# Attention values of one window group projected token-major for all heads at the start of a layer

## What is computed

```python
for l in range(DEPTH):                                  # DEPTH = 2
    h = rms_norm(x, g_mix[l])
    z = h @ w_in[l]
    qa, ka, va, ga, ub, vb, qc, kc, vc, gates = split_cols(z)
    # A: retention on qa, ka, va, ga (4 heads of 128)
    # B: causal spatial gating on ub, vb
    # C: 3 window groups x 4 heads x 128, with normed q and k
    for gi, (win, dil) in enumerate(((128, 1), (512, 4), (2048, 16))):
        o, lse = dilated_window_attention(qc[:, :, gi], kc[:, :, gi], vc[:, :, gi], win, dil)
        ...
    wts = softmax(stack(lses)); yc = sum(wts * outs)
    x = x + merged(gates, ya, yb, yc) @ w_o[l]
    x = x + SwiGLU(rms_norm(x, g_ffn[l]))
```

## Time and profile before

| | |
|---|---|
| time, median of 3 runs | 1905.05 us (1904.66 to 1905.68) |
| time of the profiled execution | 1904.88 us |
| its span in the profile | 1903.1 us |
| busy: PE, DVE, ACT, POOL | 1889.8, 1241.8, 850.4, 96.9 us |
| clock granted to TensorE, mean | 1.0 of full speed |
| read from and written to HBM | 291.79 and 77.66 MB |

### The profile page before, as it was taken

The page is one execution under the profiler, slowest core; times in us unless marked ns, Lnnn a source line. Parts: engine busy times, 40 slices in busy tenths (PEclk is TensorE's granted clock), DMA queues, the critical chain, the costliest instruction groups (busy, mean ns, idle before and its releaser), DMA issues. The chain is left out here.

```text
span 1903.1 us, 26512 instructions
## 1 busy us (share of the span) xinstructions
PE 1889.8 (99%) x10600; PEld 1696.9 (89%) x10600; DVE 1241.8 (65%) x1617; ACT 850.4 (45%) x1190; POOL 96.9 (5%) x148
## 2 busy tenths in 40 slices
PE   8999999999999999999999999999999999999999
PEld 7888888888888899899888888888888888998998
DVE  7767746666566786377577677566665667863775
ACT  5544444444334464155335444444443344642554
POOL 0000001111111000000000000011111110000000
PEclk9999999999999999999999999999999999999999
DMA  5322347777787455366333222577777774653663
GB/s 203 94 75 71 86 114 206 193 195 197 200 213 208 125 177 174 100 191 197 122 100 95 68 78 80 143 191 194 207 199 197 210 195 128 189 160 104 201 211 123
DMA packets 85897, 295.68 MB, mean 155 GB/s; under 512 B 20368, under 2 KB 20624, under 8 KB 84624
## 3 DMA queue, kind: packets, MB, share of 16 engines
q1 hardware_dynamic: 73104, 218.49, 37.0%
q0 software_dynamic: 12672, 75.51, 17.5%
HBM read 291.79 MB, written 77.66 MB: 194 GB/s over the span
## 5 line engine op out<-in xcount | busy, mean ns | idle before, releaser
L1076 ACT ACTIVATE w_high<-raw 128x1024 fp32r<-128x1024 f32 x396 | 418.3, 1057 | 780.1 <-PE bank L851 651.0
L1284 DVE TENSOR_TENSOR w_low<-raw,w_high 128x1024 fp32r<-128x1024 f32 x396 | 483.0, 1222 | 142.8 <-ACT w_high L1076 136.1
L851 PE MATMUL bank<-h_high,w_high 128*128 128x512 f32 x1344 | 518.7, 386 | 9.0 <-DVE h_low L1289 8.2
L851 PE MATMUL bank<-h_low,w_high 128*128 128x512 f32 x1344 | 510.1, 380 | 0.0
L851 PE MATMUL bank<-h_high,w_low 128*128 128x512 f32 x1344 | 510.1, 380 | 0.0
L851 PEld LDWEIGHTS bank<-h_high,w_high 128*128 128x128 f32 x1344 | 254.7, 190 | 45.3 <-issue 8.2
L851 PEld LDWEIGHTS bank<-h_high,w_low 128*128 128x128 f32 x1344 | 254.5, 189 | 36.2
L851 PEld LDWEIGHTS bank<-h_low,w_high 128*128 128x128 f32 x1344 | 254.7, 189 | 35.1
L851 PE MATMUL bank<-in_high,w_high 128*128 128x512 f32 x672 | 255.4, 380 | 0.0
L851 PE MATMUL bank<-in_low,w_high 128*128 128x512 f32 x672 | 254.7, 379 | 0.0
L851 PE MATMUL bank<-in_high,w_low 128*128 128x512 f32 x672 | 254.7, 379 | 0.0
(11 more groups left out here) (166 smaller groups left out, 2451.7 us busy)
## 6 DMA issues: line engine op xcount, KB each, us to landing
raw<-weights SPq DMA_DIRECT2D x325, 512.0 KB, 4.2
weight_sums<-weights POOLq DMA_DIRECT2D x108, 512.0 KB, 6.5
raw<-weight_sums SPq DMA_DIRECT2D x72, 512.0 KB, 4.1
weight_sums<-weight_sums POOLq DMA_DIRECT2D x36, 512.0 KB, 4.0
turned<-rows SPq DMA_DIRECT2D x3, 768.0 KB, 7.4
xT<-x_t SPq DMA_DIRECT2D x8, 256.0 KB, 5.7
decay_sb<-decay SPq DMA_DIRECT2D x8, 256.0 KB, 4.0
out_t<-xT SPq DMA_DIRECT2D x8, 256.0 KB, 4.5
```

The lines of the kernel that those rows point to most:

```text
L851: return pe.matmul(o, w, m, start=start, stop=stop)
L1076: act.activation(w_high[:, PART_SLOT[s], :, :], raw[:, s % RAW_SLOTS, :, :], ACT.Copy).then_inc(part_high_w.sem, 1)
L1284: dve.tensor_tensor(w_low[:, PART_SLOT[s], :, :], raw[:, s % RAW_SLOTS, :, :], w_high[:, PART_SLOT[s], :, :], ALU.subtract).then_inc(part_ ...
```

## The change

The value tiles of group 0 (v0 of each head) leave the heads. Four token-major tiles `vz` at the very start of the layer project the group-0 values of all four heads at once, into both score banks, the output bank and one of the turn banks. Once the norm is known, ACT evacuates them to `vz` in SBUF, and the `pv` of group 0 reads them there. A head has eight tiles. `pre[t+12..14]` becomes `pre[t+13..15]` for `ptrans` and `pv`; `weigh` stays at t+11, which with eight tiles to a head is the fourth tile (q0) of the following head. Keys k0 of the first head lose their exception. The norm of a layer's input is computed after the third tile, and spread after the fourth. `rq 0` and `rk 0` go ahead of the `rv` tiles, whose banks change. At the start, SP loads the second slab before the last two parts of x, and ACT and DVE split it there. POOL, which waits for the evacuation of `rq 0`, starts its sums of weights four tiles earlier. The number of tiles stays the same.

```diff
 def tiles_of_layer():
     t = []
+    t += [("vz", j) for j in range(HEADS)]
     for h in range(HEADS):
         t += [("k", h, g) for g in range(N_GROUP)] + [("q", h, g) for g in range(N_GROUP)]
-        t += [("v", h, g) for g in range(N_GROUP)]
-    t += [("rv", j) for j in range(HEADS)]
+        t += [("v", h, g) for g in range(1, N_GROUP)]
...
     for h in range(HEADS):
-        t += [("rq", h), ("rk", h), ("rg", h)] + gated(2, [h])
+        t += [("rq", h), ("rk", h)] + [("rv", j) for j in range(HEADS) if h == 0] + [("rg", h)] + gated(2, [h])
...
-            pre[t + ((2, 4, 4) if h > 0 else (3, 4, 4))[j]] += [("rowstat", "ck", h, j), ("rowstd", "ck", h, j)]
+            pre[t + (2, 4, 4)[j]] += [("rowstat", "ck", h, j), ("rowstd", "ck", h, j)]
...
-        pre[t + 7] += [("scores", h, 0), ("scores", h, 1), ("expo", h, 0), ("vtrans", "v", h, 0)]
+        pre[t + 7] += [("scores", h, 0), ("scores", h, 1), ("expo", h, 0)]
         pre[t + 8] += [("scores", h, 2), ("scores", h, 3), ("expo", h, 1)]
         post[t + 8] += [("gather", h), ("swap", h)]
         pre[t + 11] += [("weigh", h)]
-        pre[t + 12] += [("ptrans", h, 0), ("ptrans", h, 1)]
-        pre[t + 13] += [("ptrans", h, 2), ("pv", h, 0), ("ptrans", h, 3)]
-        pre[t + 14] += [("pv", h, 1), ("pv", h, 2), ("high", "yc", h), ("low", "yc", h)]
+        pre[t + 13] += [("ptrans", h, 0), ("ptrans", h, 1)]
+        pre[t + 14] += [("ptrans", h, 2), ("pv", h, 0), ("ptrans", h, 3)]
+        pre[t + 15] += [("pv", h, 1), ("pv", h, 2), ("high", "yc", h), ("low", "yc", h)]
...
-        if i < AHEAD_OF_NORM:
-            assert not pre[i] and len(BLOCKS[i]) == KT
+        if TILES[i][0] == "vz":
             steps.append(("main", i, 0, KT))
...
+            if i == AHEAD_OF_NORM:
+                steps += [("stat", "n", 0), ("rstd", "n", 0)]
+            steps += splits + later
+            if i == AHEAD_OF_NORM + 1:
+                steps += [("bcast", "n", 0), ("keep_rstd", 0), ("token_evac", "vz")]
             continue
...
+            if role == "vz":
+                return score_bank + [out_bank, turn_bank[1]]
...
-            return [stat_bank, out_bank, bank_of(base, AT["rv", 0]), score_bank[0]]
+            return [stat_bank] + score_bank + [out_bank]
...
             for n in range(KT):
                 sp.dma_start(xT[:, n, :], x_in[:, n, :]).then_inc(x_loaded[n], 16)
-            load(0, 1)
+                if n == SECOND_SLAB_AT:      # SECOND_SLAB_AT = 5
+                    load(0, 1)
...
                 if role == "rv" and j == 0:
+                    pe.wait_ge(std_ready.sem, std_ready.at(base, "cq", HEADS - 1))
+                    pe.wait_ge(score_taken.sem, score_taken.at(base, "scores", HEADS - 1, 3))
                     pe.wait_ge(low_ready.sem, low_ready.at(base, "yc", HEADS - 2))
...
+                same = [u for u in range(i) if TILES[u][0] not in TOKEN_ROLES and bank_of(base, u) is bank_of(base, i)]
+                if same and first == 0:
+                    wait_evacuated(pe, base, same[-1])
...
-                        pe.wait_ge(v_stored.sem, v_stored.at(base, "v", h, g))
+                        if g == 0:
+                            pe.wait_ge(values_ready.sem, values_ready.at(base, "vz", BLK - 1))
+                        else:
+                            pe.wait_ge(v_stored.sem, v_stored.at(base, "v", h, g))
...
+                                v = v_tok[g][:, kb, :] if g > 0 else vz[kb][:, h * P:(h + 1) * P]
-                                last = matmul(o, v_tok[g][:, kb, :], probsT[:, n, :],
+                                last = matmul(o, v, probsT[:, n, :],
```

More of the change, by code:

```diff
@@ L152 @@
     PROJECTION_EVENTS += [("slab", b[0]) for b in _bs[:-1] if LAST_BLOCK[b[0]] == (_i, b)] + [(_i,)]
-TOKEN_ROLES = ("rv", "sv")
+TOKEN_ROLES = ("vz", "rv", "sv")
 SCALED_ROLES = {"rq", "rk", "v", "rg", "su", "gate", "fgate"}
@@ L215, in schedule @@
         pre[t + 11] += [("weigh", h)]
-        pre[t + 12] += [("ptrans", h, 0), ("ptrans", h, 1)]
-        pre[t + 13] += [("ptrans", h, 2), ("pv", h, 0), ("ptrans", h, 3)]
-        pre[t + 14] += [("pv", h, 1), ("pv", h, 2), ("high", "yc", h), ("low", "yc", h)]
+        pre[t + 13] += [("ptrans", h, 0), ("ptrans", h, 1)]
+        pre[t + 14] += [("ptrans", h, 2), ("pv", h, 0), ("ptrans", h, 3)]
+        pre[t + 15] += [("pv", h, 1), ("pv", h, 2), ("high", "yc", h), ("low", "yc", h)]
     for h in range(HEADS):
-        t = AT["rq", h]
-        post[t] += [("rotate", "rq", h)]
-        post[t + 1] += [("rotate", "rk", h)]
+        post[AT["rq", h]] += [("rotate", "rq", h)]
+        post[AT["rk", h]] += [("rotate", "rk", h)]
+        t = AT["rg", h] - 2
         pre[t + 3] += [("rscore", h, m) for m in range(2)]
@@ L278, in schedule @@
         later = [("split_low", s) for s in todo if FIRST_USE[s] > i]
-        if i < AHEAD_OF_NORM:
-            assert not pre[i] and len(BLOCKS[i]) == KT
+        if TILES[i][0] == "vz":
+            assert not pre[i] and not post[i]
             steps.append(("main", i, 0, KT))
[L282 to L285, removed]
-            continue
[L287 to L293, removed]
+            if i == AHEAD_OF_NORM:
[3 more added lines that the diff above has]
+                steps += [("bcast", "n", 0), ("keep_rstd", 0), ("token_evac", "vz")]
+            continue
+        if i in AFTER_NORM:
+            w = 1 + AFTER_NORM.index(i)
             steps += [("main", i, 0, KT)] + splits + later
@@ L298, in schedule @@
                       ("main", i + 1, BCAST_AT, KT)]
-        elif i - 1 not in AFTER_NORM[1:]:
+        elif i - 1 not in AFTER_NORM:
             steps.append(("main", i, 0, len(BLOCKS[i])))
@@ L309 @@
 STAT_AT, BCAST_AT = 3, 6
-AFTER_NORM = (AT["k", 0, 0], AT["fgate", 0, 0])
+AFTER_NORM = (AT["fgate", 0, 0],)
 AHEAD_OF_NORM = 2
+SECOND_SLAB_AT = 5
 STEPS = schedule()
@@ L389, in build @@
                       over("values_low", in_low_at + 10 * row_bytes, [P, 2, SEQ], F32)]
+        vz_rows = [over("first_values_high", in_high_at + 4 * row_bytes, [P, 2, SEQ], F32),
+                   over("first_values_low", in_low_at + 4 * row_bytes, [P, 2, SEQ], F32)]
+        vz = [vz_rows[m // 2][:, m % 2, :] for m in range(BLK)]
         ret_v = [ret_v_rows[m // 2][:, m % 2, :] for m in range(BLK)]
@@ L601, in wait_turn_bank @@
         def wait_turn_bank(pe, base, n):
+            if n == 1:
+                pe.wait_ge(values_ready.sem, values_ready.at(base, "vz", BLK - 1))
             if n < 2:
@@ L886, in by_token @@
                     k = 2 * j + kk
+                    if role == "vz":
+                        pe.wait_ge(low_ready.sem, low_ready.at(base, "h", 0, k))
+                        seen_inputs.add(("h", 0, k))
                     wh, wl = (in_turn(w[:, PART_SLOT[slab], 4 * kk:4 * kk + 4, :].rearrange("p c n -> p (c n)"))
@@ L889, in by_token @@
                     for b in range(BLK):
-                        if role == "rv" and k == 0 and b == BLK - 1:
-                            pe.wait_ge(score_taken.sem, score_taken.at(base, "scores", HEADS - 1, 2))
                         if role == "sv" and k == 0 and b == BLK - 1:
@@ L957, in score_target @@
                 n = S_USERS.index(user)
+                if user[0] == "rscore" and user[1] == 0:
+                    pe.wait_ge(values_ready.sem, values_ready.at(base, "rv", 2))
                 if n >= 2:
@@ L1091, in _ @@
                 high_of_x(h_high[:, n, :], n, first_gain)
-            split(0, 1)
+                if n == SECOND_SLAB_AT:
+                    split(0, 1)
             for n in range(KT):
@@ L1160, in _ @@
                         for b in range(BLK):
-                            dst, func = (ret_v[b], ACT.Copy) if role == "rv" else (sg_v[:, b, :], ACT.Gelu_apprx_tanh)
+                            dst, func = {"vz": (vz[b], ACT.Copy), "rv": (ret_v[b], ACT.Copy),
+                                         "sv": (sg_v[:, b, :], ACT.Gelu_apprx_tanh)}[role]
                             act.activation(dst, token_bank(base, role)[b][:, :], func, scale=rs[:, b:b + 1]).then_inc(
@@ L1668, in _weights @@
                     k, at = 2 * t[1] + i // 4, i % 4 * P
-                    values = w_in[layer][k * P:(k + 1) * P, of((t[0], 0)):of((t[0], 0)) + HEADS * P]
+                    col = of(("v", 0, 0) if t[0] == "vz" else (t[0], 0))
+                    values = w_in[layer][k * P:(k + 1) * P, col:col + HEADS * P]
                     values = values.reshape(P, 2 * P, 2).transpose(0, 2, 1).reshape(P, HEADS * P)
```

8 lines of the change are left out of this document (2 added, 6 removed).

## The result

| | before | changed | ratio (95% interval) |
|---|---|---|---|
| time, median | 1905.37 us (4 runs) | 1932.12 us (4 runs) | 1.014 (1.0128 to 1.0152) |
| span of the profiled execution | 1903.1 us | 1929.4 us | |

The change costs 26.8 us. The forecast had the direction and the wait, and missed 17 us: the time lies outside its range.

A forecast was written before the change was run, and what follows sets the result against it. PE's own instruction stream plus the start was taken to bound the kernel: 1904.88 - 3.5 (turning of v0) + 13.6 (six waits at stat q0) = 1915.0 us, with a range of 1906.5 to 1921.

The forecast's parts named there:

- Turned values: PE no longer turns v0: eight groups of four transposes go, 0.44 us each, 3.5 us saved.
- The chain from the end of q0 to its square: ACT and DVE links delay q0's square to 7.45 us; PE waits 2.27 us at stat q0, six times, 13.6 us.
- Next in line: After the wait, q1's square is done at about 14 us, before PE's stat q1 at 15.2; holds by 1 us.
- A: The moment at which PE has issued the last matmul of q0, from which the chain is counted.
- Rival 3: A further deadline slips (stat q1, pair swap or a DVE evacuation): up to 1 us more at six heads, 1915 to 1921; chance 0.12.
- The table load: ACT's load between the slab's high part and shift_exp begins only after the operation ahead ends; 1.37 us in each chain.
- The clock: PE's clock expected full, also in the six waits of 2.27 us; no cost in the sum.
- rival 4: The clock falls in the six waits, costing at least 1.9 us each: 1926 us; chance 0.07.
- The start, zero: First matmul stays at 8.24 us and nine matmuls still run at half clock; the changed start is worth nothing.
- Nothing late by POOL: POOL's sums, begun four tiles sooner beside the last head's swap, end in no PE wait; no cost.

The follow-up runs named there:

- experiment 1: Changed kernel with weigh moved from pre t+11 to post t+10, behind the evacuation of the k2 tile: 1903.18 us, 0.9991 of before.
- the filled kernel: Changed kernel with eleven extra matmuls on PE, whose product nothing reads, ahead of stat q0 in heads 1 to 3: 1917.91 us, ratio 1.0066 to before.
- experiment 8: Changed kernel with weigh in post t+10 and POOL's sums of weights begun at the evacuation of rg 0 instead of rq 0: 1903.40 us, 0.9988 of before.
- FILL = 6, 4 and 2: Changed kernel with six, four or two extra matmuls on PE ahead of stat q0 in heads 1 to 3: 1918.2, 1923.6 and 1928.7 us.
- experiment 4: Changed kernel with rowstat and rowstd of k0 moved to pre t+3, behind weigh, for heads 1 to 3: 1923.91 us, ratio 1.0096 to before.

## Why the prediction was right or wrong

- **Turned values, -3.5 us: right.** The group of value transposes has 64 where it had 96. Take every place where other work stands between two 512- or 256-column matmuls, and of the distance between these two what is more than one matmul: in PE's timeline this adds up to 131.7 us in experiment 1 and to 135.4 before, 3.7 less.
- **The chain from the end of q0 to its square: right.** It took 7.14 us against 7.13, and the wait of 2.2 us is 2.37 between starts, against 2.27, at the six places named. The 0.1 more is the last handover: PE resumes 0.15 us after the square's end (109.97 to 110.12), where my estimate was 0.06. In the sum: 6 x 2.37 = 14.2 for 13.6.
- **Next in line: right.** q1's square ended 13.6 us after A, which the forecast had at about 14, and PE had no wait at stat q1. Rival 3 did not occur there.
- **The table load: the row was right.** 103.90 is where the split ends and the load begins, and the exponential begins 0.02 us after the load. The Trainium skill (ScalarE: Activation LUTs, What ACT_TABLE_LOAD costs) gives a drain of about 1380 ns more for a switch. This case's traces don't agree: these rows leave no gap for it.
- **The clock: the step that failed.** The forecast took the clock as full in the waits, so the term for it in the sum was nothing. It had no ground for that: the text itself said that waits of 0.5 us don't exclude a fall for 2.3 us, and still gave rival 4 a chance of 0.07 and left it out of the range. The clock fell behind five of six waits, which cost 13.4 us by the profile and 14.2 against the filled kernel; the range ended 11 us short. Rival 4 had the mechanism and the place right and the size too small, 11.4 us: it priced all six at 1.9 and called that the least. Two falls cost 1.7, three 3.4, and one place had none.
- **The start, zero: right as far as it can be told.** The first matmul came at 8.21 us. Six matmuls ran at half clock where there had been nine, but 9 to 13 in the other profiles of this start, so this is chance. (The view of windows gives 1.00 for this stretch in every profile; only the distance between the matmuls shows the half clock there.)
- **Nothing late by POOL: wrong.** "End in no PE wait that I can find": the swap of the last head came late. In the changed kernel's profile DVE waits 8.15 us for it and PE loses 0.5 us. PE needs the result two tiles later, which is why so little came of it.
- **The 26.3 us between the profiles:** -3.5 (values), +14.2 (six waits), +0.4 (the second one-column matmul behind each wait starts 0.075 us late), +13.4 (half clock), +0.5 (last head), -0.6 (the start), and +0.9 for the stretch from the last matmul's start to the end of the span (4.6 against 3.7). That makes 25.3; most of the 1.0 left lies in steps of 0.1 to 0.3 us at places outside the windowed attention. Another 0.3 us of the time lies outside the span: 2.1 us where it was 1.8.
- **Open:** experiments 1 and 8 should have come to 1901.4 to 1901.6 and came to 1903.2 and 1903.4. About 0.6 of it is the base, a profiled execution of 1904.9 where the medians beside them were 1905.3 to 1905.5. Another 0.3 is the time outside the span, 2.1 or 2.2 us in every run of both and 1.7 or 1.8 in every run of before beside them. In their profiles the stretch behind the last matmul's start is 0.7 and 1.1 us longer than in that of before. But it is 3.7 us, as before, in the kernels with FILL = 6, 4 and 2 and in that of experiment 4, so the change doesn't force it. The half-clock start of experiment 8 has thirteen matmuls for nine (0.8 us). What sets these was not settled.

## What to carry to other kernels

In a kernel that one engine bounds, follow what each moved step is put *in front of* on every in-order engine: here an exponential and its table load slid ahead of a square for which PE waits, a tile later than before. Price a new wait of TensorE twice, once as time and once as clock: for six waits of 2.2 us in this kernel the second price (13.4 to 14.2 us) was about as large as the first (14.2 us). Where no row shows what a wait of the forecast length does to the clock, the range has to hold both cases. Where a wait can't be removed, check whether a shorter one or independent matmuls in it keep the clock.

## What the runs showed of the hardware

- One wait of TensorE of 0.9 us left the granted clock at 2.4 GHz in 6 places of 6. Behind one of 1.3 us it fell to 1.2 GHz in 3 of 6, behind 1.5 us in 6 of 6, 1.8 us in 6 of 6, 2.2 us in 5 of 6; behind three waits of 0.8, 0.4 and 0.2 us within 3.4 us in 3 of 6. Each count is of one execution. Ahead of each, PE had run without a pause, and behind or between them came one-column matmuls. Whether the clock would fall without these was not tested.
- The fall shows after PE has resumed, not in the wait (1.00 in 107.6 to 109.8 us, 0.59 in 109.8 to 112.0 us). The half clock lasted 3.4 or 6.8 us and cost 1.7 or 3.4 us.
- A read of 4 KB landed 2.0 to 2.3 us after its issue beside the ordinary loads, 7.5 and 8.8 us beside POOL's 512 KB transfers, and 3.2 us once these began later.
